# A hybrid encoder step: the mixer's projections, scores and output projection in another order

## Chip, cores and metric

One core of a Trainium2 chip. The metric is the device time of one execution in microseconds, the median of the runs shown: 1239.99 us (3 runs, 1239.7 to 1240.03) before the change.

## The reference, cut to what matters

Two layers over 288 tokens (256 of a prompt, 32 new ones with a cache of 128), model width 1024, feed-forward width 2816, everything in float32:

```python
h = LN0(alpha*h + 0.5*SwiGLU_0(h))
h = LN1(alpha*h + W_o [A(h) | B(h) | C(h) | D(h)])   # the mixer
h = LN2(alpha*h + 0.5*SwiGLU_1(h))
```

The mixer reads one combined projection `h @ w_in`. A is sliding-window attention with sinks. B is sparse attention: an indexer (`relu(qi @ ki)` weighted by `wi`) scores all keys, `top_k` takes 64 per prompt query and 40 per new one, and softmax runs over those alone. C is stick-breaking attention (sigmoids and a sum over later keys, no softmax). D is latent attention: queries and keys come from low-rank latents that an RMS norm precedes, and each head's score is the sum of a 64-wide part without position and a 32-wide rotated part that all heads share on the key side:

```python
k = concatenate([kv[..., :NOPE_DIM], broadcast(kr)], -1)        # 64 + 32
s = einsum('bthd,bshd->bhts', q, k) * (NOPE_DIM + ROPE_DIM) ** -0.5
```

The projected keys and values are outputs too, beside the result.

## The kernel before

Activations lie transposed: 128 rows of a feature block by 288 tokens. A float32 product is made of three matmuls on rounded halves (`three`, L437 to L439: high weight by high input, high weight by low input, low weight by high input). Weights arrive in chunks of up to 128x2048 through three buffers; SyncE loads them in order, ScalarE writes the rounded high half (`high_part`, L967), VectorE the low half (`low_part`, L1254; `low_half`, L1267, in two parts), and GpSimd the low halves of five chunks of the output projection and what follows (`low` in its block, L384). A chunk's load waits for the low half of the chunk three before it, and its high half for TensorE's use of that chunk. Every engine runs its own list in the written order, and semaphores join the lists.

A layer is a feed-forward, a norm, the mixer, a norm, a feed-forward, a norm. In the feed-forward behind the mixer TensorE starts with two chunks at once for each of the eight input blocks (`first_two`), so that it follows the norm block by block. A norm takes the sums over features by matmuls with a matrix of ones (`stats_most`, `stats_rest`, L530 to L546), and closes with eight filler matmuls (L551).

The mixer of before, in TensorE's order: the token-major projections (values, `wi`, the rotary key) from 72 matmuls of 484 columns (L800 to L804); then 15 feature-major tiles of 24 matmuls each (`project`), in the order kc, qc, qi, (ki, kb), ka, qa, cq, ckv, qb, with small work after certain tiles (`after_tile`): rotary swaps, C's scores and sums, C's weighted values, the indexer's logits after tile 9, A's scores after tile 11. After the tiles: A's transposes (L664 to L667), D's queries (`d_queries`), A's weighted values (L700 to L713), D's keys and values, one eighth of the output projection (24 matmuls, L437 to L439), B's scores, another eighth, and so on in turns with D's scores, transposes and weighted values. `scores` (L624 to L645) first writes the masks into the banks of PSUM, then adds the products.

VectorE works out the index scores (`indexer`, L1457, L1459) after tile 9, and `choose` takes the top 64 and 40 in 16 rounds of MAX8 (L1493) and MATCH_REPLACE8 (L1494), eight on 128x256, five on 128x160 and three on 64x128. They stand in its list in four parts, the last nine rounds behind D's rotation (`rope_d`). The last call turns the result into B's mask `hide_b` (L1498, three operations); B's scores need it. For each of A, B and D, `largest` takes the row maxima (L1505 to L1507), ScalarE's `softmax` the exponentials and sums (L1056 to L1065), `divide` scales them (L1523 to L1529), TensorE transposes, and `copy_t` copies to SBUF.

For D, 96 rows of each head are put together in `qd` and `kd`: 64 by two copies of ScalarE each (L1182, L1183, L1189, L1190), 32 by copies of GpSimd (L403, L416). The latent's key half (`ckv_low`, L1595) is made before D's keys are projected.

Of the kernel before, what the change touches and what calls it, by code (L numbers as in the profile page):

```python
# [5 lines left out]
ALU = mybir.AluOpType  # L6
# [7 lines left out]
P = 128  # L14
# [30 lines left out]
LAYER_CHUNKS = FFN1_AT + FFN_CHUNKS  # L45

# [10 lines left out]

def chunk_width(local):
# [4 lines left out]
    if MIX_AT <= local < MIX_AT + TM_CHUNKS:  # L63
        return 4 * V_TOK
    if MIX_AT + TM_CHUNKS <= local < WO_AT - 1:
        return 8 * P * len(FM_TILES[local - MIX_AT - TM_CHUNKS])
# [11 lines left out]
T_KC, T_QC, T_QI, T_KK, T_KA, T_QA, T_CQ, T_CKV, T_QB = 0, 2, 4, 6, 7, 8, 10, 12, 13  # L78
# [6 lines left out]
SCORES_AT = (4, 0, 0)  # L85
T_BANK = ((4, 5, 6, 7), (6, 7, 4, 5), (0, 1, 2, 3))
WO_ROW = {"A": 0, "B": 1, "C": 2, "D": 3}
PV_BANK = (4, 4, 6, 0)
WO_PARTS = (("A", "C"), ("B", "D"))

SLOT = {"A": lambda h: h, "D": lambda h: h, "C": lambda h: h, "B": lambda h: 2 * (h % 2) + h // 2}


def encoder_program(nc, weights, x_in, ln_gb, rms_g, sinks, k_cache, v_cache, tables, mats, masks, kr_tables,
                    out_y, out_k, out_ka, out_v, out_vs, out_va):
    ctx = ExitStack()
    with ctx:
# [74 lines left out]
        neg_m, e = sb("neg_m", [P, 9], offset=e)  # L172
        sums, e = sb("sums", [P, 9], offset=e)
# [64 lines left out]
        d_rotated = sem("d_rotated")  # L238
# [4 lines left out]
        scores_ready, max_ready = sem("scores_ready"), sem("max_ready")  # L243
        exp_ready, probs_ready = sem("exp_ready"), sem("probs_ready")
# [32 lines left out]
        def down_bank(q):  # L277

            return (6, 4)[q % 2]

# [69 lines left out]
        def _(pool):  # L350
# [13 lines left out]
            def square_sums(n):  # L364

                for q in (1, 2):
                    pool.wait_ge(zsq_ready, 5 * n + q + 1)
                    pool.tensor_tensor(zsqsum[:, :, :], zsqsum[:, :, :], squares(n, q), ALU.add).then_inc(zsq_added, 1)  # L368
                    pool.wait_ge(zsq_added, 2 * n + q)
                if n % 3 == 1:  # L370
                    pool.tensor_tensor(zsqsum[:, 0, :], zsqsum[:, 0, :], zsqsum[:, 1, :], ALU.add).then_inc(zsqsum_ready, 1)
                    return
# [14 lines left out]
            for l in range(DEPTH):  # L387
# [4 lines left out]
                pool.dma_start(v_past[:, :], v_cache[l]).then_inc(cache_landed, 16)  # L392
                pool.wait_ge(values_copied, 3 * (l + 1))
# [4 lines left out]
                pool.wait_ge(roped, ROPED * l + 2)  # L398
# [16 lines left out]
                for h in range(4):  # L415
                    link(pool.tensor_copy(qd[64:96, h, :], qd_rot[32 * h:32 * h + 32, :]))  # L416
# [1387 lines left out]
```

## Time and profile before

| | |
|---|---|
| median of 3 runs | 1239.99 us |
| the profiled execution: its own time, its span | 1239.98 us, 1238.2 us |
| TensorE busy | 1168.6 us (94%) |
| VectorE, ScalarE, GpSimd busy | 656.6 (53%), 524.0 (42%), 110.0 us (9%) |
| mean granted TensorE clock | 0.977 |
| chain that ended last | PE 85%, DVE 9%, ACT 3% |

The table says that TensorE is nearly always at work over the whole. The question is which stretches make the rest, so the waits and the busy time by stretch are read, not the averages. The granted clock is a share of 2.4 GHz: 1.00 is that, 0.50 is 1.2 GHz.

### The profile page before, as it was taken

How to read it: one execution, taken by the hardware profiler on the slowest of the kernel's cores; microseconds unless marked ns; L12 is line 12 of the kernel's file. 1: busy time of each engine (PE TensorE's matmuls, PEld its weight loads, DVE VectorE, ACT ScalarE, POOL GpSimd, SP SyncE). 2: the span in 40 equal slices, each digit the busy share in tenths (PEclk: the TensorE clock that was granted, in tenths of full speed). 3: DMA queues.
4: the chain of work that ended last, by engine and by line, in shares of the span. 5: the costliest groups of instructions: out<-in, count | busy, mean ns of one | idle time of the engine just before them, and what ended most of it. 6: DMA issues, size and time to landing. Idle time of an engine off the chain costs nothing.

```text
span 1238.2 us, 20493 instructions
## 1 busy us (share of the span) xinstructions
PE 1168.6 (94%) x8558; PEld 1125.9 (91%) x8558; DVE 656.6 (53%) x847; ACT 524.0 (42%) x715; POOL 110.0 (9%) x104
## 2 busy tenths in 40 slices
PE   7999999999777999999999999999987989999996
PEld 6999999799667999999999999997886879999996
DVE  5445444556754745544474554437467565554444
ACT  5443333453633633443363444335444435444432
POOL 1000001001343000000100000020106120000001
PEclk8999999999988999999999999999997999999998
DMA  8544445332332344445444444445223125454431
GB/s 320 169 165 156 152 167 173 116 129 96 111 102 69 123 156 167 166 153 166 166 142 160 166 169 153 165 156 178 70 83 130 61 68 175 165 169 161 162 119 39
DMA packets 28098, 176.93 MB, mean 143 GB/s; under 512 B 3264, under 2 KB 4352, under 8 KB 10240
## 3 DMA queue, kind: packets, MB, share of 16 engines
q1 hardware_dynamic: 26288, 170.18, 40.1%
q0 software_dynamic: 1744, 5.81, 1.5%
q8 instruction: 49, 0.80, 0.3%
q14 instruction: 17, 0.14, 0.0%
HBM read 171.72 MB, written 4.25 MB: 142 GB/s over the span
## 4 chain that ended last, share of the span: by engine, by line
PE 85%; DVE 9%; ACT 3%; issue 2%; DMA 1%; SPq 0%; DVEq 0%; ACTq 0%
PE ps L437 24%; PE ps L439 24%; PE ps L438 24%; PE ps L476 1%; PE ps L481 1%; PE ps L477 1%; ACT w_high L967 1%; DVE score L1494 1%; PE ps L664 1%; PE ps L800 1%; PE ps L801 1%; PE ps L804 1%; DVE best L1493 1%; DVE score L1459 1%; PE ps L636 1%
## 5 line engine op out<-in xcount | busy, mean ns | idle before, releaser
L437 PE MATMUL ps<-x_high,w_high 128*128 128x288 f32 x1648 | 494.2, 300 | 12.6 <-DVE x_low L1653 5.9
L438 PE MATMUL ps<-x_low,w_high 128*128 128x288 f32 x1648 | 489.5, 297 | 0.0
L439 PE MATMUL ps<-x_high,w_low 128*128 128x288 f32 x1648 | 489.2, 297 | 0.0
L1254 DVE TENSOR_TENSOR w_low<-raw,w_high 128x2048 fp32r<-128x2048 f32 (+3 forms) x152 | 332.5, 2188 | 272.2 <-ACT w_high L967 271.3
L967 ACT ACTIVATE w_high<-raw 128x2048 fp32r<-128x2048 f32 (+2 forms) x167 | 304.9, 1827 | 117.8 <-PE ps L439 116.1
L437 PEld LDWEIGHTS ps<-x_high,w_high 128*128 128x128 f32 x1648 | 312.3, 190 | 15.2 <-DVE x_low L1653 6.1
L438 PEld LDWEIGHTS ps<-x_low,w_high 128*128 128x128 f32 x1648 | 312.9, 190 | 0.6
L439 PEld LDWEIGHTS ps<-x_high,w_low 128*128 128x128 f32 x1648 | 312.8, 190 | 0.0
L437 PE MATMUL ps<-hid_high,w_high 128*128 128x288 f32 x704 | 208.4, 296 | 0.0
L438 PE MATMUL ps<-hid_low,w_high 128*128 128x288 f32 x704 | 208.0, 295 | 0.0
L439 PE MATMUL ps<-hid_high,w_low 128*128 128x288 f32 x704 | 207.9, 295 | 0.0
L986 ACT ACTIVATE silu_g<-ps 128x288 f32<-128x288 f32 x88 | 36.1, 410 | 305.0 <-PE ps L439 305.0
L438 PEld LDWEIGHTS ps<-hid_low,w_high 128*128 128x128 f32 x704 | 132.3, 188 | 0.0
L437 PEld LDWEIGHTS ps<-hid_high,w_high 128*128 128x128 f32 x704 | 132.2, 188 | 0.0
L439 PEld LDWEIGHTS ps<-hid_high,w_low 128*128 128x128 f32 x704 | 132.1, 188 | 0.0
L1290 DVE SCALAR_TENSOR_TENSOR gated<-silu_g,ps 128x288 f32<-128x288 f32 x88 | 39.9, 453 | 158.5 <-ACT silu_g L986 158.5
L368 POOL TENSOR_TENSOR zsqsum<-zsqsum,zsq 128x576 f32<-128x576 f32 x10 | 16.5, 1653 | 804.8 <-ACT zsq L1025 804.8
L384 POOL TENSOR_TENSOR w_low<-raw,w_high 128x512 fp32r<-128x512 f32 x40 | 50.7, 1296 | 57.5 <-ACT w_high L967 57.4
L1278 DVE TENSOR_TENSOR hid_low<-gated,hid_high 128x288 f32 (+1 forms) x88 | 40.2, 457 | 1.0
L975 ACT ACTIVATE hid_high<-gated 128x288 f32 (+1 forms) x88 | 38.4, 437 | 0.8 <-DVE gated L1290 0.8
L1038 ACT ACTIVATE x_high<-z,gb 128x288 fp32r<-128x288 f32 x35 | 18.8, 537 | 28.1 <-DVE z L1361 27.9
L476 PE MATMUL ps<-x_high,w_high 128*128 128x288 f32 x96 | 26.5, 298 | 3.4 <-DVE x_high L1369 3.4
(278 smaller groups left out, 989.2 us busy)
## 6 DMA issues: line engine op xcount, KB each, us to landing
raw<-weights SPq DMA_DIRECT2D x139, 1024.0 KB, 4.9
raw<-weights SPq DMA_DIRECT2D x16, 768.0 KB, 4.3
raw<-weights SPq DMA_DIRECT2D x4, 968.0 KB, 4.8
raw<-weights SPq DMA_DIRECT2D x6, 512.0 KB, 3.8
out_k<-kT POOLq DMA_DIRECT2D x2, 864.0 KB, 4.6
raw<-weights SPq DMA_DIRECT2D x2, 640.0 KB, 4.0
hT<-x_in SPq DMA_DIRECT2D x4, 288.0 KB, 5.3
out_y<-hT SPq DMA_DIRECT2D x4, 288.0 KB, 2.1
```

The lines of the kernel that those rows point to most:

```text
L384: ins = pool.tensor_tensor(wl[:, n], r[:, n], wh[:, n].bitcast(F32), ALU.subtract)
L437: pe.matmul(out, wh, xh, start=first, stop=False, skip_group_check=True)
L438: pe.matmul(out, wh, xl, start=False, stop=False, skip_group_check=True)
L439: return pe.matmul(out, wl, xh, start=False, stop=last, skip_group_check=True)
L476: pe.matmul(out, wh[:, g, k, :], x_high[:, k, :], start=(k == 0), stop=False, skip_group_check=True)
L967: act.activation(wh, r, ACT.Copy).then_inc(high_ready, 1)
L975: act.activation(hidden(hid_high, t, m), gated[:, t % 2, :], ACT.Copy).then_inc(hid_high_ready, 1)
L986: act.activation(silu_g[:, t % 2, :], ps[:, gate_bank(t), 0:TOK], ACT.Silu).then_inc(silu_ready, 1)
L1038: act.activation(x_high[:, j, :], z[:, j, :], ACT.Identity, bias=gb[:, l, which, 1, j:j + 1]).then_inc(x_high_ready, 1)
L1254: dve.tensor_tensor(wl, r, wh.bitcast(F32), ALU.subtract).then_inc(low_ready, 1)
L1278: dve.tensor_tensor(hidden(hid_low, t, m), gated[:, t % 2, :], hidden(hid_high, t, m).bitcast(F32), ALU.subtract).then_inc(hid_low_ready, 1)
L1290: dve.scalar_tensor_tensor(out=gated[:, t % 2, :], in0=silu_g[:, t % 2, :], scalar=0.5, in1=ps[:, gate_bank(t) + 1, 0:TOK], op0=ALU.mult, ...
```

## The change

The mixer's work is put in another order. The indexer's tiles come first: `first_four` takes tiles qi, (ki, kb), ka from two chunks for each input block, as `first_two` does in the feed-forward, and the token-major projections come behind them. The logits follow at once, so `choose` starts after tile 4; its 16 rounds stand one by one between the low halves of weights. C's work moves behind tiles 8, 11 and 12, A's scores behind tile 12. D's scores are no longer made from 96 rows: `scores_d` adds a product over 64 rows (`qn`, `kn`, one copy of ScalarE each) and one over 32 rows (`qd_rot`, and the rotary key, which `key_rotation` now writes four times, once for each head). GpSimd's copies into `qd` and `kd` are gone. B's and D's scores are made one behind the other in all eight banks, and two eighths of the output projection follow them. Semaphores now tell of the scores, maxima and exponentials in two parts. In the mixer's norm the two halves of `zsum` and `zsqsum` are no longer added up: the matrix of ones takes each half by a matmul of its own, and `stats_most` stands ahead of the last tile's matmuls. The first feed-forward's last `low_half` pair moves out of the norm to its end, as the second one had it. `WO_PARTS` pairs C with A; the packing of the weights follows the order. Added lines of the two mixers, and the edits around them (removed lines of the mixers' lists are in the functions above):

```diff
-SCORES_AT = (4, 0, 0)
-T_BANK = ((4, 5, 6, 7), (6, 7, 4, 5), (0, 1, 2, 3))
+SCORES_AT = (2, 0, 4)
+T_BANK = ((4, 5, 2, 3), (0, 1, 4, 5), (0, 1, 4, 5))
...
-PV_BANK = (4, 4, 6, 0)
-WO_PARTS = (("A", "C"), ("B", "D"))
...
-SLOT = {"A": lambda h: h, "D": lambda h: h, "C": lambda h: h, "B": lambda h: 2 * (h % 2) + h // 2}
+SWAP_AT = (0, 4, 0, 6)
+D_SWAP = 1
+TM_BANK = (2, 3, 6)
+PV_BANK = (0, 4, 2, 0)
+WO_PARTS = (("C", "A"), ("B", "D"))
...
-        kd, e = sb("kd", [96, 4, KEYS], offset=e)
+        kn, e = sb("kn", [P, 2, KEYS], offset=e)
+        qn, e = sb("qn", [P, 2, TOK], offset=e)
         qd_rot, e = sb("qd_rot", [P, TOK], offset=e)
-        qd, _ = sb("qd", [96, 4, TOK], offset=e)
...
+                pool.wait_ge(roped, ROPED * l + 2)
+                pool.tensor_copy(kT[64:128, KI, 0:TOK], kT[0:64, KI, 0:TOK]).then_inc(k_shared, 1)
+                pool.tensor_copy(kT[0:64, KB, 0:TOK], kT[64:128, KB, 0:TOK]).then_inc(k_shared, 1)
...
-                kr = kT[64:96, KR, :].rearrange("p (o t) -> p o t", o=1).to_broadcast([32, 4, KEYS])
-                link(pool.tensor_copy(kd[64:96, :, :], kr))
...
+                low(l, WO_AT)
+                low(l, WO_AT + 1)
+                low(l, WO_AT + 2)
                 pool.dma_start(out_k[l, 64:96, KR, :], kT[64:96, KR, 0:TOK]).then_inc(stored, 16)
+                low(l, WO_AT + 3)
+                low(l, WO_AT + 4)
...
-                for h in range(4):
-                    link(pool.tensor_copy(qd[64:96, h, :], qd_rot[32 * h:32 * h + 32, :]))
-                pool.sem_inc(d_rotated, 1)
-                for local in range(WO_AT + 1, FFN1_AT + 1):
-                    low(l, local)
...
+                slots = [(i, g) for i in range(2) for g in range(2)]
+                nope = [(qn[head(g), i, :], kn[head(g), i, :]) for i, g in slots]
+                turned = [(qd_rot[32 * h:32 * h + 32, :], kT[32 * h:32 * h + 32, KR, :]) for h in (2 * i + g for i, g in slots)]
...
+                window_d(nope, (0, 1), False)
+                first_d(nope, (0, 1), False)
+                window_d(turned, (0,), True)
+                link(first_d(turned, (0,), True))
+                window_d(turned, (1,), True).then_inc(scores_ready, 1)
+                first_d(turned, (1,), True)
...
                     if t == 4:
...
                         pe.wait_ge(relu_ready, 3 * l + 2)
                         sample_logits(1, 0)
+                    if t == 5:
+                        key_rotation(l)
+                    if t == 8:
+                        c_scores(l)
+                    if t == 10:
+                        pe.wait_ge(relu_ready, 3 * (l + 1))
+                        swap(l, 2, SWAP_AT[2])
                     if t == 11:
+                        c_sums(l)
                         pe.wait_ge(roped, ROPED * l + 3)
...
                         pe.wait_ge(latent_squared, 2 * l + 1)
...
+                            mm = pe.matmul(ps[:, 0, 0:TOK], ones, cq_sq[:, j, :], start=(j == 0), stop=(j == 1))
...
+                    if t == 12:
+                        pe.wait_ge(c_weights_ready, l + 1)
+                        scores(0, halves(QA, KA, True), window_hidden, second_hidden, (qs[:, 0, :], kT[:, KA, :]))
+                        pe.wait_ge(latent_rstd_ready, 2 * l + 1)
+                        weighted(l, 0)
+                    if t == 14:
+                        pe.wait_ge(o_low_ready, 4 * l + 1)
                         pe.wait_ge(latent_squared, 2 * (l + 1))
...
+                        pe.matmul(ps[:, 1, 0:TOK], ones, ckv_sq, start=True, stop=True).then_inc(latent_summed, 1)
...
+                for k in range(KD):
+                    first_four(k)
+                for k in range(KD):
+                    token_major(k)
+                    if k == 1:
+                        swap(l, 0, SWAP_AT[0])
+                    if k == 4:
+                        swap(l, 1, SWAP_AT[1])
+                indexer_second_block(l)
+                indexer_first_block(l)
+                for i in range(2, FM_CHUNKS):
...
+                swap(l, 3, SWAP_AT[3])
                 pe.wait_ge(low_ready, l * LAYER_CHUNKS + local + 1)
                 pe.wait_ge(latent_low_ready, 2 * l + 1)
...
+                pe.wait_ge(latent_rstd_ready, 2 * (l + 1))
+                d_queries(0, 0)
+                d_queries(1, 1).then_inc(d_projected, 1)
+                transposes(l, 0)
+                pe.wait_ge(d_copied, 4 * l + 1)
+                d_queries(2, 0).then_inc(d_projected, 1)
                 weighted(l, 1)
...
+                pe.wait_ge(d_copied, 4 * l + 2)
+                pe.matmul(ps[:, D_SWAP, 0:TOK], swap_r, rope_x[:, 0, 0, :], start=True, stop=True).then_inc(swapped, 1)
                 pe.wait_ge(latent_low_ready, 2 * l + 2)
+                pe.wait_ge(roped, ROPED * l + 4)
...
                 pe.wait_ge(o_low_ready, 4 * l + 2)
                 d_values(4).then_inc(d_projected, 1)
                 d_values(5).then_inc(chunk_used, 1)
...
                 pe.wait_ge(roped, ROPED * (l + 1))
                 pe.wait_ge(k_shared, 2 * (l + 1))
                 pe.wait_ge(topk_done, l + 1)
                 scores(1, halves(QB, KB, True), chosen1, chosen0, (qs[:, 1, :], kT[:, KB, :]))
                 pe.wait_ge(d_copied, 4 * (l + 1))
...
+                scores_d()
+                pe.wait_ge(exp1_ready, 3 * l + 2)
+                out_projection(l, WO_AT, 0, 0, BOTH).then_inc(part_ready, 1)
+                pe.wait_ge(exp_ready, 3 * l + 2)
+                out_projection(l, WO_AT, 1, 2, BOTH).then_inc(chunk_used, 1)
+                transposes(l, 1)
+                pe.wait_ge(exp_ready, 3 * l + 3)
                 out_projection(l, WO_AT + 1, 0, 6, BOTH).then_inc(part_ready, 1)
...
                 pe.wait_ge(part_added, 4 * l + 2)
...
                 weighted(l, 2)
+                transposes(l, 2)
+                pe.wait_ge(part_added, 4 * l + 3)
+                out_projection(l, WO_AT + 1, 1, 6, BOTH).then_inc(chunk_used, 1)
+                weighted(l, 3)
+
                 out_projection(l, WO_AT + 2, 0, 4, ONE)
...
                 out_projection(l, WO_AT + 2, 0, 4, OTHER).then_inc(wo_ready, 1)
...
+                pe.wait_ge(part_added, 4 * l + 4)
+                out_projection(l, WO_AT + 2, 1, 6, BOTH).then_inc(chunk_used, 1)
+                out_projection(l, WO_AT + 3, 0, 2, BOTH).then_inc(wo_ready, 1)
                 out_projection(l, WO_AT + 3, 1, 0, BOTH, (0,)).then_inc(tile6_ready, 1)
+                stats_most(event)
...
+                softmax(l, 1, 0.125)
+                softmax(l, 2, 96 ** -0.5)
+                copy_t(l, 1)
                 high_until(base + 15)
-                softmax(l, 1, 0.125)
                 high_until(base + 16)
-                softmax(l, 2, 96 ** -0.5, between=lambda: copy_t(l, 1))
+                copy_t(l, 2)
                 out_high(l, 2)
-                copy_t(l, 2)
+                out_high(l, 3)
...
-                    if q == 3 and i == 1:
+                    if q == 3:
...
             def mixer(l):
...
+                low_until(base + 3)
                 low_until(base + 4)
+                rope_first(l, 0)
+                rope_rest(l, 0)
+                rope_first(l, 1)
+                fixed_choice()
+                low_until(base + 5)
+                rope_rest(l, 1)
+                low_until(base + 6)
                 key_rotation(l)
...
+                indexer(l, 0)
+                indexer(l, 1)
                 low_until(base + 7)
+                indexer(l, 2)
+                choose(0, 1)
+                choose(1, 2)
+                choose(2, 3)
+                choose(3, 4)
+                low_until(base + 8)
+                low_until(base + 9)
+                choose(4, 5)
+                choose(5, 6)
+                choose(6, 7)
+                choose(7, 8)
+                choose(8, 9)
+                choose(9, 10)
+                choose(10, 11)
+                dve.wait_ge(c_log_ready, l + 1)
...
                 rope_first(l, 2)
                 rope_rest(l, 2)
...
+                low_until(base + 10)
+                choose(11, 12)
+                choose(12, 13)
+                choose(13, 14)
...
+                low_until(base + 11)
+                largest(l, 0, 0.125)
+                out_low(l, 0)
+                low_until(base + 12)
...
                 divide(l, 0)
...
+                rope_first(l, 3)
+                rope_rest(l, 3)
+                copy_t(l, 0)
+                choose(14, 15)
+                choose(15, 16)
...
                 out_low(l, 1)
                 rope_d(l)
...
+                largest(l, 1, 0.125)
+                largest(l, 2, 96 ** -0.5)
+                divide(l, 1)
                 part(l, 0)
...
+                divide(l, 2)
+                copy_t(l, 1)
                 part(l, 1)
...
                 part(l, 2)
...
+                low_until(base + MIX_CHUNKS + WO_CHUNKS + 1)
                 out_low(l, 2)
```

## Rows read from the trace of the kernel before

**Rows 1.** waits of TensorE, layer 0's mixer: total us, times, longest.

```profile
PE ps L624 <- DVEq L1499: 7.2, 1, 7.2
PE ps L664 <- DVEq L1530: 5.4, 1, 5.4
PE ps L530 <- DVE zsum L1335: 4.7, 1, 4.7
PE ps L880 <- DVE x_low L1549: 1.9, 1, 1.9
PE ps L437 <- DVE x_low L1549: 1.7, 1, 1.7
```

**Rows 2.** stretch length, busy PE, PEld, DVE, ACT, POOL, granted clock, DMA share, GB/s.

```profile
229.65:402.66 173.01, 151.34 (x1076) 134.59 (x1076) 104.17 (x188) 78.28 (x147) 38.63 (x36) 0.94 0.30 102
838.75:1010.70 171.95, 151.67 (x1076) 135.00 (x1077) 103.21 (x188) 78.29 (x147) 38.66 (x36) 0.93 0.30 102
320.30:323.70 3.40, 2.86 (x14) 2.80 (x15) 3.11 (x9) 2.20 (x3) 1.54 (x3) 0.50 0.39 163
344.20:354.40 10.20, 7.80 (x34) 6.02 (x35) 4.97 (x7) 0.00 (x0) 4.49 (x4) 0.50 0.61 206
374.90:378.30 3.40, 3.40 (x18) 3.38 (x17) 0.01 (x1) 0.60 (x1) 0.00 (x0) 0.50 0.00 0
398.80:402.20 3.40, 3.40 (x9) 2.40 (x8) 0.00 (x0) 0.84 (x2) 0.00 (x0) 0.50 0.72 287
```

**Rows 3.** the same view, stretches that each hold one block of TensorE's work.

```profile
405.69:418.60 12.91, 12.91 (x96) 12.78 (x97) 10.95 (x22) 9.67 (x16) 0.00 (x0) 1.00 0.00 1
251.94:252.67 0.73, 0.73 (x7) 0.49 (x7) 0.73 (x1) 0.62 (x2) 0.00 (x0) 1.00 1.03 426
301.65:304.14 2.49, 2.43 (x27) 2.09 (x25) 2.22 (x8) 1.66 (x3) 0.00 (x0) 1.00 0.00 0
359.62:363.31 3.69, 3.63 (x39) 3.09 (x37) 2.78 (x3) 0.49 (x1) 3.05 (x3) 1.00 0.00 0
363.31:366.60 3.29, 3.29 (x34) 3.29 (x25) 2.23 (x4) 0.80 (x3) 1.94 (x2) 1.00 0.25 37
366.60:368.32 1.72, 1.72 (x16) 1.39 (x14) 1.40 (x2) 1.64 (x8) 0.00 (x0) 1.00 0.73 295
368.95:372.36 3.41, 3.40 (x40) 2.88 (x40) 1.79 (x4) 1.73 (x10) 0.00 (x0) 1.00 0.12 48
224.56:226.50 1.94, 1.94 (x11) 1.43 (x9) 0.46 (x1) 0.73 (x2) 1.48 (x2) 1.00 0.00 0
```

**Rows 4.** chain of waits, 318 to 347: start us, us, what.

```profile
331.66 0.44 DVE best L1493
...
332.64 0.44 DVE best L1493
...
337.41 0.34 DVE best L1493
...
338.19 0.34 DVE best L1493
```

**Rows 5.** all instructions of one VectorE line: duration ns min/median/max.

```profile
L1436 DVE TENSOR_TENSOR qs<-rope_a,rope_b x8: 217/222/1220, 296.0 to 937.4; 64x64 f32<-64x64 f32 x8
...
L1498 DVE TENSOR_SCALAR hide_b<-score x6: 1148/1196/1240, 342.7 to 953.9; 128x256 bf16<-128x256 f32 x2, 64x128 bf16<-64x128 f32 x2, 32x160 bf16<-32x160 f32 x2
```

**Rows 6.** busy time by stretch: softmax, division, rotation, maxima of a group.

```profile
354.60:358.16 3.56, 3.56 (x30) 3.56 (x28) 0.75 (x1) 3.56 (x19) 0.00 (x0) 1.00 0.00 0
358.34:360.56 2.22, 2.16 (x17) 1.90 (x17) 2.18 (x4) 1.77 (x1) 0.30 (x1) 1.00 0.00 0
294.38:297.20 2.82, 2.82 (x22) 2.72 (x21) 2.71 (x6) 0.52 (x2) 0.00 (x0) 1.00 0.59 166
352.25:354.50 2.25, 2.25 (x10) 2.25 (x11) 2.22 (x4) 0.00 (x0) 0.00 (x0) 0.52 0.22 91
```

**Rows 7.** waits of TensorE at the end of layer 0's second feed-forward.

```profile
PE ps L530 <- DVE zsum L1335: 1.0, 1, 1.0
```

More of the change, by code:

```diff
@@ L529, in stats_most @@
                 pe.wait_ge(zsum_ready, n + 1)
-                pe.matmul(ps[:, 2, 0:TOK], ones, zsum[:, 0, :], start=True, stop=False)
+                if n % 3 != 1:
+                    pe.matmul(ps[:, 2, 0:TOK], ones, zsum[:, 0, :], start=True, stop=False, skip_group_check=True)
+                else:
+                    for i in range(2):
+                        pe.matmul(ps[:, 4, 0:TOK], ones, zsum[:, i, :], start=(i == 0), stop=False, skip_group_check=True)
             def stats_rest(n):
@@ L584, in indexer_second_block @@
                         q, k = logits(slice(128, 256), slice(0, 256), pair, half)
-                        mm = pe.matmul(ps[:, 2 + half, 256 * pair:256 * pair + 256], q, k, start=True, stop=True,
+                        mm = pe.matmul(ps[:, 4 + half, 256 * pair:256 * pair + 256], q, k, start=True, stop=True,
                                        skip_group_check=True)
@@ L593, in sample_logits @@
                         q, k = logits(slice(SEQ, TOK), keys, pair, half)
[L594 removed]
+                        mm = pe.matmul(ps[0:32, half, at_ + lo:at_ + hi], q, k, start=True, stop=True,
                                        skip_group_check=True)
@@ L602, in indexer_first_block @@
                         q, k = logits(slice(0, 128), slice(0, 128), pair, half)
-                        pe.matmul(ps[:, 6 + half, 128 * pair:128 * pair + 128], q, k, start=True, stop=True,
+                        pe.matmul(ps[:, half, 128 * pair:128 * pair + 128], q, k, start=True, stop=True,
                                   skip_group_check=True)
@@ L643, in scores @@
                     for lo, hi, keys in ((256, 384, slice(TOK, KEYS)), (384, 416, slice(SEQ, TOK))):
-                        for h, (q, k) in enumerate(slots):
-                            mm = pe.matmul(ps[32 * h:32 * h + 32, b0, lo:hi], q[:, SEQ:TOK], k[:, keys],
-                                           start=False, stop=True, skip_group_check=True)
+                        for (i, g), (q, k) in zip(slots, pairs):
+                            rows = 32 * (2 * g + i)
+                            mm = pe.matmul(ps[rows:rows + 32, b0, lo:hi], q[:, SEQ:TOK], k[:, keys],
+                                           start=False, stop=last, skip_group_check=True)
@@ L719, in halves @@
                         for g in range(2) for i in range(2)]
-            heads_d = [(qd[:, h, :], kd[:, h, :]) for h in range(4)]
             def window(bank):
@@ L1394, in norm @@
                     scale(j)
-                    if which == 0 and j in (4, 5):
-                        low_half(l * LAYER_CHUNKS + MIX_AT + 1, j - 4)
                 low(KD - 2)
```

472 lines of the change are left out of this document (223 added, 249 removed).

## Prediction

> **What bounds the kernel now.** I read the page first: TensorE is busy for 94% of the span and leads the chain of waits for 85% of it, so nothing off TensorE pays by itself. The view of its waits, cut to layer 0's mixer, then says what the other 6% is [rows 1]. Five waits come there to 7.2 + 5.4 + 4.7 + 1.9 + 1.7 = 20.9 us, all ended by VectorE: B's scores wait for the top-k mask, A's transposes for the division, the norm's sums for `zsum`, and two steps for small low halves. The reader should see that the feed-forwards are not in it. The busy time by stretch gives the second loss [rows 2]: from the mixer's first matmul to the norm's last sum, layer 0 takes 173.01 us and layer 1 171.95. In four stretches the granted clock is 0.50 (1.2 GHz); each stands at or behind one of the waits, and TensorE is busy in them for 2.86 + 7.80 + 3.40 + 3.40 = 17.46 us, of which half, 8.7 us, would not be needed at 2.4 GHz. So layer 0's mixer holds 173.0 - 20.9 - 8.7 = 143.4 us of work, and 29.6 us can go at most.
>
> **The change, part by part.** *Work added to TensorE.* In the norm's sums five products with ones become eight: each of the four in 224.56:226.50 takes 1.94 / 4 = 0.485 us [rows 3], so +1.5. D's scores: from 96 rows they take 3.69 with masks and samples, A's from pairs of 64 rows 2.49 [rows 3]. If the two heads of a pair run side by side, as A's shorter time says, two parts cost about as much as one of 96 rows, and a stop between them and twice the samples add some 0.5. The bounds are 0 and +3.0 (the 32-row parts do not pair, and the second part costs the whole again); I take 0.5, A's row being the nearest. The rotary key written four times: 0.73 before [rows 3]; 0 to +2.2, and 0.3 taken, since the four go to different columns, as D's samples do. In all 143.4 + 2.3 = 145.7 us. The first tiles cost nothing new: 12.91 us for eight input blocks of twelve matmuls in `first_two` [rows 3] is two pairs of tiles at 6.5.
>
> *The top-k.* A round on 256 columns takes 332.64 - 331.66 = 0.98 us, one on 160 338.19 - 337.41 = 0.78 [rows 4]; with three short ones at about 0.7, the sixteen are 8 x 0.98 + 5 x 0.78 + 3 x 0.7 = 13.8 us. Fourteen now lie in the projections, where TensorE has tiles of 3.2 us one behind the other and VectorE is idle for a good part (over the mixer busy 104.17 of 173.01 [rows 2]). The low halves of the weights stand behind them: by the lists, that of the chunk of tiles 10 and 11 is ready some 9 us ahead of its use, the next ones 12 and more. So they cost nothing, and the 7.2 us wait goes. Without this cover each round would cost its 0.7 to 0.98 us. The two last rounds and the three mask operations stay, ahead of `ckv_low`, and that is the new joint.
>
> I set the four joints where TensorE is next to wait, each as a race between its queue and the other engines'.
>
> Joint 1, A's probabilities. TensorE has two tiles behind C's weighted values, 2 x 3.29, a sum of squares 0.5, a swap 1.0 and D's first queries 12/24 x 3.29 = 1.65: 9.7 us. Beside it ScalarE takes C's output and two reads of the latent (about 1.2), a 1280-wide high half (1.3), and the exponentials, 3.56; VectorE divides in 2.22 + 0.5 for the sinks [rows 6]: 8.8 us. Ahead by 0.9, so the 5.4 us wait goes.
>
> Joint 2, `ckv_low`. From there TensorE has the transposes 1.72, D's last queries 0.8, A's weighted values 3.41 and a swap 0.5: 6.4. VectorE, which starts 0.9 earlier, has the last rotation 2.82, 1.7 for three small operations, two rounds 1.4, and three mask operations. These took 1.15 to 1.24 us each in every one of six cases [rows 5]; yet `qs` shows 0.22 us at its median and 1.22 at its worst, and GpSimd was at work both in that case and in all six. In the new order GpSimd waits at this point for the next chunk's high half. So I take 0.3 each: 6.8 - 0.9 = 5.9, ahead by 0.5. At 1.2 each it is 9.5 - 0.9 = 8.6, and TensorE waits 2.2.
>
> The Trainium skill (SBUF — State Buffer, "SBUF: two separate sides") says that VectorE and GpSimd share one pair of ports as an exclusive lock that the first one holds for its whole instruction. The trace agrees in `qs` (0.22 against 1.22 us). By that rule GpSimd's low halves, which now run three in a row beside B's and D's softmax, could hold VectorE up there, which my sum leaves out.
>
> Joint 3, B's probabilities. TensorE has D's scores 4.2 and two eighths of the output projection, 2 x 3.29: 10.8. Against it B's maxima 2.25, exponentials 3.56, D's maxima at most 2.25 in between, division 2.22 [rows 6]: 10.3. Ahead by 0.5; D's own chain ends well inside the next 8 us. Before, D's had 3.29 + 1.72 + 3.41 = 8.4 us of cover [rows 3], hence the 1.7 us wait.
>
> Joint 4, the sums. The last `z` addition and `zsum` take 1.6 to 2.0 us behind the last whole eighth, and half an eighth, 1.65 us, covers them: 0.3 us stays of 4.7. Semaphores, D's scores (which wait about 0.2 for ScalarE's copies of D's values behind two high halves) and the joint above leave 1.0 us of waits in all.
>
> GpSimd's copies into `kd` and `qd` and two of ScalarE's were hidden and are worth nothing. The chunks of the output projection are ready 2 us and more ahead. With no wait over a microsecond left, no stretch at half clock should be left either. So the mixer takes 145.7 + 1.0 = 146.7 us: 26.3 less in layer 0 and 25.3 less in layer 1, 51.6 together. Against it, the first feed-forward's end now has the `low_half` pair, as the second one's has, where TensorE waits 1.0 us for `zsum` [rows 7]: 2 x 1.0. The norm's shorter list on VectorE is not on the path. Gain 49.6 us. The profiled execution took 1239.98 us (span 1238.2 and 1.8 around it), the median is 1239.99, so the forecast is 1190.4, called 1190.
>
> **Rivals.** *The joints are missed* (0.22). Three are ahead by less than 1 us in a sum of many terms. For it speaks the lock above and that every number is a mean. A miss costs its wait, and the half clock behind it: the 1.7 us wait was followed by 3.40 us of work at 0.50, 1.7 us more [rows 1, 2]. Joint 2 with masks at 1.2 us costs 2.2 + 1.7 = 3.9 a layer, 1198; two more misses of 1.7 + 1.7 make 10.7 a layer, 1212.
>
> *The rounds push the projections* (0.05). VectorE's list is strict, so twelve more rounds, 12 x 0.88 = 10.6 us, could hold up the low halves of tiles 10 to 14, and then TensorE waits 10.6 us and has a stretch like that of 10.2 us at half clock (about 4 us): 14.6 a layer, 1220. Against it: the slack of 9 us.
>
> *Slower than before* (0.03): the narrow work, now one long piece from the last tile to the last weighted values (some 45 us at full clock) and on into the output projection, is not enough activity, and the clock stays at 0.50 to the mixer's end, 60 us of work. Price +60 a layer, 1190 + 120 = 1310; it decides once over 50 us of work per mixer runs at 0.50. Against it: blocks of 96-row scores and of weighted values show 1.00 [rows 3]. The Trainium skill (TensorE: Matmul & The Clock Gate, "What's actually happening") says that the default is the throttled clock and that activity releases it, and says nothing of narrow tiles there.
>
> **How the numbers follow.** The forecast holds 0.70, from 1184 (nothing added and no wait, both mixers at 143.4) to 1196. The range reaches from 1181 (some term too dear by a us or two a layer) into the missed joints, to 1207, and leaves out some 0.15 on the slow side and 0.03 below. What this measurement can tell from no change is 0.2%, 2.5 us. All cases but the third rival are faster: 0.96; within 0.2%: 0.01; slower: 0.03.
>
> **What would show it.** TensorE's waits in a mixer should sum to under 2 us, none for the mask, and the granted clock be 1.00 throughout it. The mask operations should take about 0.3 us. D's scores should take 4.2 us, the mixer 147 and the end of each first feed-forward 1 us more. A wait of over 1 us for `ckv_low`, the division or a weight's low half shows rival one or two, a long stretch at 0.50 without waits the third. The forecast is wrong if TensorE's work at full clock is more than 150 us a mixer, or if its waits come back at places that I have not named.

## The result, and the profile after

The changed kernel takes 1187.88 us (median of 4 runs, 1187.75 to 1188.94) against 1239.85 us for the kernel before (4 runs): a ratio of 0.9584 (95% interval 0.9567 to 0.9601), 52 us less. A later set of runs, made with the experiments, gave 0.9588 (0.9575 to 0.9600). The forecast was 1190.

TensorE's waits over the whole span come first, as in [rows 1]: total us, times, longest.

```profile
PE ps L457 <- DVE x_low L1761: 5.9, 1, 5.9
PE ps L496 <- DVE x_high L1458: 3.5, 3, 1.2
PE ps L551 <- DVE zsum L1420: 3.1, 3, 1.1
PE ps L457 <- DVE w_low L1339: 2.5, 1, 2.5
PE ps L871 <- DVE x_high L1458: 2.3, 2, 1.2
PE ps L554 <- DVE zsum L1426: 1.0, 2, 0.5
```

All five waits of [rows 1] are gone; of the mixer's own only the last line is left, 0.5 us in each layer. The first and fourth line stand at the kernel's start, the second and fifth at the entries of stages, and they were there before. New is part of the third: 3 waits where [rows 7] was the one of its kind in layer 0.

The busy time by stretch (columns as in [rows 2]): layer 0's mixer, layer 1's, D's scores, the sums' first two products and their last six, and the stretch at half clock at the kernel's start (the other one left is in its last 7 us, as before the change).

```profile
229.97:375.61 145.64, 144.75 (x1131) 129.71 (x1132) 95.87 (x188) 76.12 (x145) 35.17 (x30) 1.00 0.33 111
812.84:958.49 145.65, 144.75 (x1131) 129.69 (x1132) 95.87 (x188) 76.13 (x145) 35.18 (x30) 1.00 0.33 111
330.58:335.20 4.62, 4.50 (x70) 3.63 (x68) 3.68 (x6) 3.09 (x15) 4.54 (x5) 1.00 0.47 142
370.03:370.89 0.86, 0.86 (x5) 0.70 (x5) 0.86 (x1) 0.00 (x0) 0.86 (x1) 1.00 0.20 80
372.70:375.61 2.91, 2.91 (x14) 2.19 (x13) 0.46 (x1) 1.17 (x3) 0.00 (x0) 1.00 0.73 225
18.80:22.20 3.40, 3.40 (x17) 3.40 (x16) 3.39 (x3) 1.74 (x1) 0.00 (x0) 0.50 1.01 385
```

The granted clock is 1.00 through both mixers. Against [rows 2] they are 173.01 - 145.64 = 27.4 and 171.95 - 145.65 = 26.3 us shorter; the first feed-forwards' ends take 1.08 and 1.00 us back: 51.6 of the 52.2 us between the spans (1238.2 and 1186.0). The other 0.6 us lie at the start, where the half-clock stretch was shorter in this execution; that has nothing to do with the change.

VectorE's mask operations and row maxima, answering to [rows 5] (duration ns min/median/max):

```profile
L1585 DVE TENSOR_SCALAR hide_b<-score x6: 224/231/294, 322.9 to 906.4; 128x256 bf16<-128x256 f32 x2, 64x128 bf16<-64x128 f32 x2, 32x160 bf16<-32x160 f32 x2
...
L1599 DVE TENSOR_SCALAR neg_m<-top_s x8: 331/439/574, 331.5 to 919.6; 128x4 f32<-128x4 f32 x4, 128x5 f32<-128x5 f32 x4
```

The mask now takes a fifth of the time. The second row is a loss: an operation on 128x4 takes up to 574 ns, where A's two, made while GpSimd is idle, take 170 to 172. It is taken up below.

### The profile page after: what moved, and what is told of

Its sections match the earlier page's. It is cut to its first block, busy times and chain, and to the rows that moved or that the text cites. A ratio compares the mean times of both kernels' runs of the same rounds, so it can differ in the third digit from the quotient of the medians.

```text
span 1186.0 us, 20683 instructions
## 1 busy us (share of the span) xinstructions
PE 1155.4 (97%) x8670; PEld 1115.7 (94%) x8670; DVE 646.6 (55%) x851; ACT 520.7 (44%) x711; POOL 103.7 (9%) x92
## 4 chain that ended last, share of the span: by engine, by line
PE 94%; DVE 3%; ACT 1%; DMA 1%; issue 0%; SPq 0%; DVEq 0%; ACTq 0%
PE ps L457 26%; PE ps L458 26%; PE ps L459 26%; PE ps L496 1%; PE ps L501 1%; PE ps L497 1%; PE ps L889 1%; PE ps L887 1%; PE ps L888 1%; PE ps L871 1%; PE ps L876 1%; PE ps L872 1%; PE ps L585 1%; PE ps L731 1%; ACT w_high L1056 1%; DMA raw<-weights 1%
## 5 line engine op out<-in xcount | busy, mean ns | idle before, releaser
L457 PE MATMUL ps<-x_high,w_high 128*128 128x288 f32 x1584 | 474.1, 299 | 8.4 <-DVE x_low L1761 5.9
L459 PE MATMUL ps<-x_high,w_low 128*128 128x288 f32 x1584 | 468.6, 296 | 0.0
L458 PE MATMUL ps<-x_low,w_high 128*128 128x288 f32 x1584 | 468.2, 296 | 0.0
L457 PEld LDWEIGHTS ps<-x_high,w_high 128*128 128x128 f32 x1584 | 299.3, 189 | 9.6 <-DVE x_low L1761 5.9
L459 PEld LDWEIGHTS ps<-x_high,w_low 128*128 128x128 f32 x1584 | 299.2, 189 | 0.0
L458 PEld LDWEIGHTS ps<-x_low,w_high 128*128 128x128 f32 x1584 | 298.8, 189 | 0.3
L496 PE MATMUL ps<-x_high,w_high 128*128 128x288 f32 x96 | 26.5, 298 | 3.5 <-DVE x_high L1458 3.5
```

Of the source, the lines that this page charges most:

```text
L457: pe.matmul(out, wh, xh, start=first, stop=False, skip_group_check=True)
L458: pe.matmul(out, wh, xl, start=False, stop=False, skip_group_check=True)
L459: return pe.matmul(out, wl, xh, start=False, stop=last, skip_group_check=True)
L496: pe.matmul(out, wh[:, g, k, :], x_high[:, k, :], start=(k == 0), stop=False, skip_group_check=True)
```

## Experiments

"Layer 0's mixer" is here the time from its first product to the end of the norm's fillers: 147.5 us in the changed kernel, 174.9 before. Beside the experiments the changed kernel took 1187.66 us and the kernel before 1238.1 to 1238.7 (medians); differences of times are taken against these.

**One, the place of the top-k** (in the changed kernel `choose(4, 5)` to `choose(15, 16)` are taken out and one call put in):

```diff
                 rope_d(l)
+                choose(4, 16)
                 largest(l, 1, 0.125)
```

> The changed kernel with twelve of the sixteen top-k rounds moved back behind D's rotation, in one block, as most of them stood before; everything else stays changed. My theory: the gain of the first joint comes from where the rounds stand in VectorE's list. The twelve take 4 x 0.98 + 5 x 0.78 + 3 x 0.7 = 9.9 us and the mask 0.3 (each of three operations about 0.23) behind a start at 327.2 in layer 0, so B's scores, which TensorE reaches at 327.5, can start at about 338: a wait of 10 to 11 us, and a stretch of 3 to 7 us of work at 0.50 behind it, 2 to 4 us. That is +12 to +15 a layer, 1212 to 1218; if the mask operations are at 1.2 us again beside GpSimd's low halves, some 3 more a layer (to 1224). Rival: what pays is that C's, A's and D's work has another order, and the place of the rounds is nearly off the path (VectorE has room): 1188 to 1191.

Measured: 1215.26 us, ratio 0.9814 (0.9799 to 0.9829). The waits, and the stretch at half clock behind them:

```profile
PE ps L652 <- DVEq L1586: 10.5, 1, 10.5
```

```profile
334.00:344.30 10.30, 5.00 (x23) 3.45 (x25) 4.75 (x22) 0.00 (x0) 4.14 (x4) 0.50 0.58 204
```

10.5 us of wait and 2.5 us of work at half speed are 13.0, and layer 0's mixer is 12.9 longer. In the changed kernel the place of these rounds alone is worth half of the whole gain, and the first theory holds in its number.

**Two, the norm's new sums in the kernel before:**

```diff
-                out_projection(l, WO_AT + 3, 1, 0, BOTH, (1,)).then_inc(chunk_used, 1)
                 stats_most(event)
+                out_projection(l, WO_AT + 3, 1, 0, BOTH, (1,)).then_inc(chunk_used, 1)
...
+                    for i in range(2):
+                        pe.matmul(ps[:, 4, 0:TOK], ones, zsum[:, i, :], start=(i == 0), stop=False, ...)
```

> The kernel before with one part of the change alone: in the mixer's norm the halves of zsum and zsqsum are not added up (each is taken by its own matmul with ones), and the sums stand ahead of the last tile's matmuls. My theory: the parts are separate joints and their prices add. The 4.7 us wait for zsum falls to about 0.5, the 3.4 us stretch at 0.50 at the norm goes (1.7), and three more matmuls with ones cost 1.5: 4.2 + 1.7 - 1.5 = 4.4 a layer, 1231. Rival: the wait is made by something later in VectorE's list (the last part additions), and comes back one instruction on: 1237 to 1241, with the same idle time at another matmul. Rival two: the half-clock stretch stays, since it is not the wait that makes it: 1234 to 1235.

Measured: 1236.87 us, ratio 0.9991 (0.9981 to 1.0), a span of 1236.1. The expected 9 us did not come.

```profile
PE ps L538 <- DVE zsum L1353: 2.1, 1, 2.1
```

```profile
395.00:398.40 3.40, 3.40 (x15) 3.26 (x14) 1.80 (x2) 0.44 (x1) 0.35 (x1) 0.50 0.29 43
```

By the medians it is 1238.22 - 1236.87 = 1.35 us, 0.7 a layer; the profiled execution's two mixers are 1.3 and 0.6 shorter. The wait fell from 4.7 to 2.1 and not to 0.5, and the half clock stayed. In the trace TensorE reaches the sums at 392.06 while VectorE is still a low half behind: it ends one at 392.13, then adds to `z` and to `zsum` until 394.01. From its second addition to `z` to the end of `zsum` VectorE needs 5.0 us in either order (389.00 to 394.01 here, 364.86 to 369.90 in the changed kernel), but TensorE has 3.1 us of work beside it in the old order and 4.7 in the new one. So my sum for this experiment had a hole, and the parts are not separate joints.

**Three, the reverse: the old norm in the changed kernel.**

> The changed kernel with the mixer's norm as before: the halves of zsum and zsqsum are added up on VectorE and GpSimd, five products with ones and not eight, and the sums stand behind the last tile's matmuls. In the kernel before, the new norm alone brought its wait from 4.7 to 2.1 us, kept the half-clock stretch there, and added 1.5 us of work. My theory: in the new order VectorE is not behind any more when the last whole eighth ends, so the old norm waits only for the two additions and one low half: zsum is ready at about 374.0 where TensorE is free at 371.8, a wait of 2.2 us, less 1.5 us of products: +0.7 a layer, +2.4 where a half-clock stretch follows: 1189 to 1193. Rival: the new norm is worth what the old wait was, 4.7 us and the half clock, less 1.5: +5 a layer, 1197 to 1198. Rival two: the old norm is no worse (the 1.5 us of work outweighs the wait): 1185 to 1188.

Measured: 1193.84 us, ratio 0.9627 (0.9612 to 0.9642).

```profile
PE ps L553 <- DVE zsum L1417: 3.1, 1, 3.1
```

```profile
375.20:378.60 3.40, 3.23 (x7) 2.38 (x8) 0.47 (x2) 0.54 (x2) 0.00 (x0) 0.50 0.84 289
```

A wait of 3.1 for 0.5, 1.6 us of half clock, 1.3 us of products saved: +2.9 a layer by these, +2.8 in layer 0's mixer. The time is just past the expected 1189 to 1193, as the wait is 3.1 and not 2.2. By the medians the new norm is worth 3.1 us a layer here (1193.84 - 1187.66) and 0.7 in the old order. The wait isn't what differs: it moves by 2.6 us in either order (4.7 to 2.1, 3.1 to 0.5), 1.3 a layer once the products are paid. The half clock is: in the old order its 3.4 us stretch stays with either norm, here it comes with the old norm alone. It doesn't even come each time: two of the five runs took 1190.15 and 1191.10 us, at a mean granted clock of 0.996 and 0.994 where the others have 0.991, and there the norm is worth 1.2 and 1.7 us a layer.

**Four, all rounds in one block:** `choose(0, 16)` right behind `indexer(l, 2)`, in place of the sixteen calls.

> The changed kernel with all sixteen top-k rounds in one block right behind the last index score, ahead of the low halves of the weights that they stand between in the changed kernel. My theory: the splitting into single rounds matters, since the low half of the chunk of tiles 10 and 11 is ready only 8.2 us ahead of its use and the twelve moved rounds take about 10.8 us (partly in idle time of VectorE): 2.7 us late, with a wait of that size and perhaps a stretch at 0.50 of 1.7 us: +2.7 to +4.4 a layer, 1193 to 1197. Rival: VectorE has so much idle time between the tiles that the block is caught up before TensorE's tile 10: 1187 to 1189, and the trace shows no new wait.

Measured: 1195.47 us, ratio 0.9655 (0.9640 to 0.9671).

```profile
PE ps L457 <- DVE w_low L1339: 2.6, 1, 2.6
```

The wait is the predicted one, 2.6 us for the low half of tiles 10 and 11, in both layers; layer 0's has no half-clock stretch behind it and that mixer is 2.9 longer, layer 1's has one of 3.4 us and is 4.3 longer. So the slack that the prediction leaned on ("some 9 us") was there but not twice over: splitting the rounds among the low halves is needed.

**Five, D's scores away from B's:** `scores_d()` moved behind `out_projection(l, WO_AT, 1, 2, BOTH)`.

> The changed kernel with D's scores moved behind the two eighths of the output projection, no longer right behind B's. My theory: D's scores and the two eighths together are what hides B's softmax, and the two eighths and the transposes what hides D's. TensorE then reaches the first eighth's bank while B's exponentials still read it (wait 2.8 to 3.3 us), and later D's softmax has only B's transposes ahead of it (2 to 3.5 us), with a half-clock stretch of 1.7 us behind at least one: +7 to +10 a layer, 1202 to 1208. Rival: the other blocks of the output projection fill in and the order of these two does not matter: 1187 to 1190.

Measured: 1211.56 us, ratio 0.9775 (0.9759 to 0.9790).

```profile
PE ps L731 <- DVE z L1743: 4.8, 1, 4.8
PE ps L457 <- ACT prob L1145: 3.5, 1, 3.5
```

```profile
334.70:341.50 6.80, 6.02 (x25) 6.05 (x26) 0.05 (x1) 2.46 (x14) 3.73 (x4) 0.50 0.64 226
351.80:358.60 6.80, 4.50 (x21) 4.47 (x22) 6.01 (x11) 3.98 (x13) 0.00 (x0) 0.50 0.00 0
```

The mechanism is the expected one, the size is over it: 8.2 us of waits and (6.02 + 4.50) / 2 = 5.3 us of half clock are 13.5, and layer 0's mixer is 13.2 longer. Behind each wait come 6.8 us at 0.50 in layer 0, not the 3.4 that I had reckoned. In layer 1, with the same waits, the stretches are 3.4 and 6.8 us and hold 3.41 and 3.51 us of work, so the half clock costs 3.5 us, and that mixer is 11.6 longer.

**Six and seven, why the mask is fast.** In the changed kernel GpSimd gets five, then nine additions more; they write a buffer that is no longer read. They stand ahead of its store of the keys and so ahead of all its low halves, not just ahead of the rotary key's store as the expectation says:

```diff
+                for _ in range(5):
+                    link(pool.tensor_tensor(relu_l[:, 0:512], relu_l[:, 512:1024], relu_l[:, 512:1024], ALU.add))
                 pool.dma_start(out_k[l, :, 0:KR, :], kT[:, 0:KR, 0:TOK]).then_inc(stored, 16)
                 low(l, WO_AT)
```

> The changed kernel, with five additions on 128x512 added to GpSimd's list just ahead of its store of the rotary key, so that GpSimd works while VectorE makes B's mask; they write a buffer that nobody reads any more. Nothing that TensorE needs soon waits for GpSimd there. Theory one (shared port, an operation is held up while GpSimd works): the six mask operations take about 1.2 us each as before the change and not 0.22, the latent's key half comes 2 to 3 us late, and TensorE waits 2 to 2.5 us for it, perhaps with a half-clock stretch: +4 to +8 in all, 1192 to 1196. Theory two (the 1.2 us of before was a property of the mask operation or of its operands, and the new order changed that): the mask stays at 0.22 to 0.3 us and the time within 1 us of 1187.9.

Measured with five: 1194.10 us, ratio 0.9645 (0.9630 to 0.9659). The time fits theory one, but not by its mechanism: the additions ended at 325.66, the mask began at 325.74 and took 1.13 us for all three. What was held up stood ahead of it. Of VectorE, in time: start us, us, ...

```profile
320.72 1.27 DVE L1525 TENSOR_TENSOR qs<-rope_a,rope_b 64x64 f32<-64x64 f32 x2
322.00 1.64 DVE L1527 TENSOR_TENSOR qT<-rope_a,rope_b 128x576 f32<-128x576 f32 x1
...
325.74 1.13 DVE L1587 TENSOR_SCALAR hide_b<-score 128x256 bf16<-128x256 f32 x3
```

So the mask was still to be tested, and nine additions reach over it.

> As the kernel with five extra GpSimd additions, but nine of them, so that they last through B's mask and the latent's key half; in the run with five the additions ended just before the mask began, VectorE's rotation beside them took 1044 and 1636 ns in place of 217 and 757 ns, and the mask stayed at 0.22 to 0.55 us. Theory one (what VectorE does from SBUF to SBUF with two operands, or a mask operation, is held up for as long as a GpSimd operation lasts): the mask operations now take 1.0 to 1.25 us each (+2.8 us) and the latent's key half up to 1.2 us more, so TensorE's waits there grow from 1.15 to 3.5 to 5 us a layer: 1198 to 1203. Theory two (the mask of before was slow for a reason of its own, like the order of the operations or the memory it lay in): the mask stays at 0.22 to 0.3 us, and the time within 2 us of the run with five additions, 1194.

Measured: 1211.78 us, ratio 0.9781 (0.9765 to 0.9796), past the 1203 of theory one. VectorE, and under it GpSimd:

```profile
325.53 3.36 DVE L1587 TENSOR_SCALAR hide_b<-score 128x256 bf16<-128x256 f32 x3
329.04 1.32 DVE L1711 TENSOR_TENSOR ckv_low<-kT,ckv_high 128x416 fp32r<-128x416 f32 x1
330.29 0.74 DVE L1645 TENSOR_TENSOR x_low<-ps,x_high 128x576 fp32r<-128x576 f32 x1
330.95 5.46 DVE L1534 TENSOR_TENSOR rope_a<-rope_x,tab 128x288 f32<-128x288 f32 x1
336.45 0.46 DVE L1536 TENSOR_TENSOR rope_b<-ps,tab 128x288 f32<-128x288 f32 x1
```

```profile
324.41 5.50 POOL L433 TENSOR_TENSOR relu_l<-relu_l 128x512 f32<-128x512 f32 x5
330.21 0.88 POOL L434 DMA_DIRECT2D out_k<-kT  x1 [0.30 <-POOL relu_l L433]
331.11 6.43 POOL L411 TENSOR_TENSOR w_low<-raw,w_high 128x512 fp32r<-128x512 f32 x5
```

Theory two has fallen: the mask takes 1.02 to 1.18 us an operation in layer 0 as soon as GpSimd works beside it. In layer 1 the first of the three got in ahead, with 0.29 us, and it was GpSimd's addition that took 1.19 us in place of 1.04; the other two took 0.95 and 1.09. What took the time past theory one is `rope_a`, 5.46 us where it takes 0.45 in the changed kernel (at 325.78): it stood through GpSimd's next four operations. TensorE waits 3.7 us for `ckv_low` and 3.0 for the rotated queries, each with a half-clock stretch of 6.8 us; layer 0's mixer is 12.3 longer.

**Eight, the same in the kernel before:** GpSimd's low halves are held until the mask is done.

```diff
+                pool.wait_ge(topk_done, l + 1)
                 for local in range(WO_AT + 1, FFN1_AT + 1):
                     low(l, local)
```

> The kernel before with GpSimd's low halves of the output projection's chunks held until the top-k is done, so that GpSimd is idle while VectorE makes the mask; nothing else is changed. Theory one (VectorE's mask operations are held up by GpSimd, also in the kernel before): the six mask operations take 0.22 to 0.3 us in place of 1.15 to 1.24, B's scores start 2.8 us earlier, and the 7.2 us wait falls to 4.4: -2.8 a layer, 1232 to 1234; the low halves, 4.9 us later, have 25 us before they are used. Theory two (the mask is slow in itself in the old order): the mask stays near 1.2 us and the time within 1 us of before; if the later low halves hold up other work of VectorE or TensorE, slower by 1 to 5.

Measured: 1232.36 us, ratio 0.9958 (0.9943 to 0.9972), span 1229.1, 9.1 less.

```profile
L1499 DVE TENSOR_SCALAR hide_b<-score x6: 224/230/293, 341.7 to 946.7; 128x256 bf16<-128x256 f32 x2, 64x128 bf16<-64x128 f32 x2, 32x160 bf16<-32x160 f32 x2
```

```profile
PE ps L625 <- DVEq L1500: 4.4, 1, 4.4
```

Theory one. By the medians, 1238.65 - 1232.36 = 6.3 us: one line gives back an eighth of what the whole change does. (The profiled execution is among the fastest; two of the six runs took 1235.7 and 1235.95.) In it the wait for the mask is 2.8 us shorter in each layer, and the stretch behind it 6.8 us and not 10.2. Elsewhere the half clock came both ways: in layer 0 the stretch at A's transposes grew from 3.4 to 6.8 us, and the one behind D's 1.7 us wait is gone. In all, TensorE has 14.4 us of work at half clock in that mixer where it had 17.5. Smaller waits moved by less than 1 us either way.

**Nine, the moved `low_half` pair alone, in the kernel before.**

> The kernel before with one part of the change alone: the first feed-forward's last low_half pair moves out of the norm to the feed-forward's end. My theory: it costs what I priced it at, a wait of 1.0 to 1.1 us for zsum at each first feed-forward's end, and gives nothing back in the norm, whose VectorE list is not on the path: +2.0 to +2.2, ratio about 1.002, with two more waits of that line in the trace. Rival: the norm's entry (1.15 to 1.18 us) becomes shorter by as much, or the pair was on the path in the norm: no change or faster.

Measured: 1242.42 us, ratio 1.0023 (1.0013 to 1.0033). Five waits for `zsum` in place of three, the two new ones 0.84 and 0.80 us (1.0 to 1.1 expected), and the norm's entry unchanged at 1.27: the edit brings the priced waits and nothing for them. The time doesn't show that price, though. Four of the eleven runs took 1238.4 to 1239.6 us at a mean granted clock of 0.978 to 0.980, seven 1242.2 to 1243.6 at 0.971 to 0.973, and the profiled one is of the first group: its span is 1.2 us under the kernel before's, with 30.2 us of work at half clock in the two mixers where that one has 35.9. Two groups 4 us apart, each at its own mean clock, hide an edit of 2 us.

**Ten to twelve, a better order at the feed-forwards' ends.** First `zsum` ahead of the low half:

```diff
-                            low_half(after, 1)
                             dve.wait_ge(z_ready, 5 * n + 4)
                             dve.tensor_tensor(zsum[:, 0, :], zsum[:, 0, :], z[:, 6, :], ALU.add).then_inc(zsum_ready, 1)
+                            low_half(after, 1)
```

> The changed kernel, with zsum placed ahead of the second low_half call at the ends of the feed-forwards. My theory: the wait of 1.0 us for zsum that TensorE shows three times (1.1, 1.0, 1.0) is the one low half that stands ahead of it in VectorE's list, and goes at each place where zsum is the last to come; the low half is not needed for microseconds: -2.5 to -3, 1185. Rival: the low half that is moved is then late for the next tiles (first tiles of the mixer or the feed-forward wait instead): 1187.5 to 1189, with a wait for x_low or the weights' low half in place of zsum.

Measured: 1187.00 us, ratio 0.9589 (0.9576 to 0.9602): no gain that can be told. The waits for `zsum` went, but TensorE then waited for GpSimd:

```profile
PE ps L568 <- POOL zsqsum L402: 2.0, 3, 0.7
```

```profile
L402 POOL TENSOR_TENSOR zsqsum<-zsqsum,zsq x4: 803/1659/1663, 224.6 to 1171.7; 128x288 f32<-128x288 f32 x4
```

The hold goes both ways: now GpSimd's addition takes 1659 ns beside VectorE's low half. Then the low half behind the last addition to `z`, with the changed kernel unedited on the same chip:

```diff
-                            low_half(after, 1)
                             dve.wait_ge(z_ready, 5 * n + 4)
...
+                    elif at_ == 7 and n % 3 != 1:
+                        low_half(after, 1)
```

> The changed kernel with the second low_half call at the feed-forwards' ends behind the last addition to z, so that it stands behind zsum and also does not run beside GpSimd's last addition to zsqsum. In the kernel with zsum first alone, that addition took 1657 ns beside the low half, and TensorE's wait of 1.08 us for zsum became one of 0.65 us for zsqsum. My theory (VectorE and GpSimd hold each other up, in both directions): the addition now takes about 1.0 us and the wait falls to 0 to 0.2 us at three places, with nothing new behind it: -2.5 to -3.2 against the changed kernel, about 1185, ratio 0.956 to 0.957. Rival: the 1657 ns are GpSimd's own, or the low half comes late for the mixer's second chunk: a wait of 0.5 us or more stays or comes back there, and the time is within 1 us of the changed kernel.

> The changed kernel once more, unedited, as the measure for the kernel with the half weight behind the last addition, on the same chip. Both theories expect a ratio to the kernel before of 0.957 to 0.960, as in its first runs.

Measured: 1184.28 us (1183.54 to 1185.20), ratio 0.9564 (0.9551 to 0.9576), against 1187.66 us (1186.36 to 1188.48), ratio 0.9588, for the changed kernel.

```profile
L402 POOL TENSOR_TENSOR zsqsum<-zsqsum,zsq x4: 794/798/803, 222.5 to 1167.1; 128x288 f32<-128x288 f32 x4
```

The addition takes 798 ns and no wait for `zsum` or `zsqsum` is left at these three places. VectorE's own addition to `zsum` had been held up there too: 1046 ns beside GpSimd's in the changed kernel, 457 here. The medians differ by 3.4 us, and no run of the one reaches a run of the other. This version beats both kernels.

## Why the prediction was right

*The limit.* The forecast took the mixer's waits and its half clock as what can go [rows 1, 2], and they went. The mixer after is 145.6: 145.1 of work and 0.5 of waits, where 145.7 and 1.0 were predicted. These two terms, twice 0.6 + 0.5, are 2.2 of the 2.5 us by which the forecast was too slow.

*Work added.* The eight products with ones take 0.86 + 2.91 = 3.8 us, against five at 0.485: +1.3 (predicted 1.5). D's scores take 4.6 (4.2): the two parts cost a little more than one of 96 rows, and far less than twice. The rotary key written four times takes 0.77, as good as nothing more than the 0.73 of [rows 3] (0.3).

*The mask* at 0.3 us an operation is the term on which joint 2 hung, and its reason held: 224 to 294 ns with GpSimd idle, 0.95 to 1.18 us beside it, and the one line of experiment eight does the same in the kernel before.

*The top-k.* Right in place and size: moving twelve rounds back costs 12.9 us in layer 0's mixer, and one block of them costs the low half's 2.6 us. Of the 27 us a layer, the place of the rounds makes about 13 and the norm about 3, each taken back out of the changed kernel (experiments one and three). The rest is some 11 us by subtraction. A's transposes, the two small low halves and the half clock behind them are the likely parts; no run took them apart, and a part's worth depends on what stands around it.

*The joints.* Joint 1: the division ends at 317.3, the transposes start at 318.6, ahead by 1.2 (0.9). Joint 2: ahead by 0.3 (0.5), the tightest. Joint 3: the division ends at 339.3, the transposes start at 341.7, ahead by 2.4 (0.5); what I had counted for D's maxima in between did not hold B's division up that long. Joint 4: a wait of 0.5 (0.3). D's scores waited 0.06 (0.2).

*The joints missed* (the first rival) did not happen. I had given each miss its wait and 1.7 us of half clock. Experiment five shows that this price holds in some places only: its two misses cost 5.3 us of half clock in layer 0 and 3.5 in layer 1 behind the same waits. Two misses came to 13.2 and 11.6 us, where three had been put at 10.7, mostly because their waits were 3.5 and 4.8 us and not 1.7 to 2.2. So the rival's far end of 1212 was no bound; the range was right by the forecast, not by this term.

*The rounds push the projections* is refuted by the trace of the change and shown real by experiment four: 8 us of slack, and it takes the splitting to stay inside. *The half clock over narrow work* is refuted: 1.00 throughout both mixers. That no stretch at half clock is left where no wait is over a microsecond came true as well, with luck in it: waits of 0.7 and 0.4 us were followed by one of 3.4 us in layer 0 of experiment six.

*The low halves at the first feed-forwards' ends* cost 1.08 and 1.00 us, as said (1.0 each). The prediction took that wait as the price of the move. Experiments ten to twelve show that it was a matter of order and of the other engine, and could be had back.

## What to carry to other kernels

Where one engine is busy for 94%, list its waits and its half-clock stretches for one stage, add them up, and ask of each wait what stands ahead of the awaited instruction in the other engine's list. What is long and has its inputs early (here the top-k) belongs, in small pieces, into the idle time of an earlier stage. Price a joint by its wait and the half clock behind it together, and don't add up gains of single edits: the norm's new sums took 2.6 us off a wait in either order, but gave 0.7 us a layer in one and 3.1 in the other, by the half clock behind. Look at single runs as well as at medians, since the runs of one and the same kernel (experiment nine's) fell into two groups 4 us apart, with the granted clock lower in the slower one.

## What the runs showed of the hardware

*VectorE and GpSimd hold each other up, by operand.* With GpSimd at work, VectorE's operations from SBUF to SBUF with two tensors or a scalar (`qs`, `qT`, `hide_b`, `ckv_low`, `neg_m`) don't end before the GpSimd operation that runs when they come up: the small ones end 0.02 to 0.15 us behind it, `ckv_low` 0.46 and `qT` 0.62. `qs` on 64x64 took 1.04 us in place of 0.22. Those with an operand in PSUM (`rope_b`, `x_low`, the copies) and MAX8 with its replacement kept their times. In the changed kernel GpSimd's low halves meet the row maxima, which the prediction left out. The instructions of VectorE and of GpSimd there:

```profile
331.51 0.56 DVE L1599 TENSOR_SCALAR neg_m<-top_s 128x4 f32<-128x4 f32 x1
331.98 0.68 DVE L1605 TENSOR_REDUCE top_s<-ps 128x4 f32<-128x512 f32 x1
...
332.93 0.48 DVE L1599 TENSOR_SCALAR neg_m<-top_s 128x5 f32<-128x5 f32 x1
```

```profile
329.55 7.55 POOL L411 TENSOR_TENSOR w_low<-raw,w_high 128x512 fp32r<-128x512 f32 x6
```

The reductions from PSUM run through; only the 128x4 operation stretches. The Trainium skill (SBUF — State Buffer, "SBUF: two separate sides") gives the pair of ports to whichever starts first, for that whole instruction. The runs agree on the lock and on both directions of it (1659 against 798 ns on GpSimd). They differ from it at one place: `rope_a`, put down as started at 330.95 and so ahead of GpSimd's first at 331.11, lost to four GpSimd operations in a row, 5.46 us. Why it lost each time is open; in layer 1 of the same run it took 0.62 us and `qd_rot`, two operations later, 5.62.

*The half clock behind a wait varies.* The changed kernel's mixers, with waits of 0.5 us at most inside them, have no stretch at 0.50. But the same wait doesn't always bring one, nor one of the same length: 2.6 us in experiment four had none in layer 0 and 3.4 us in layer 1, 0.4 and 0.7 us in experiment six had 3.4 us in layer 0 and none in layer 1, and behind the 10.5 us of experiment one stood 10.2 and 13.7 us. So half-clock stretches can be priced over many joints, not for one. What decides in one case was not tried.
